# Mixture-of-experts kernel: experts in pairs, full-precision products on column tiles, twelve ring slots

## What is computed

```
h = silu(x @ w_gate) * (x @ w_up)          # x: 80 x 1024, the weights 1024 x 1024, float32
out[rows] += gate * score * (h @ w_down)
```

## Time and profile before

| | |
|---|---|
| median of 3 runs | 2026.26 us (2024.73 to 2031.66) |
| profiled execution | 2036.07 us, span 2034.3 us |
| mean granted clock of TensorE in it | 0.911 of full speed |
| moved by DMA | 519 MB, 255 GB/s over the span |

### The profile page before, as it was taken

The page is one execution under the profiler, slowest core; times in us unless marked ns, Lnnn a source line. Parts: engine busy times, 40 slices in busy tenths (PEclk is TensorE's granted clock), DMA queues, the critical chain, the costliest instruction groups (busy, mean ns, idle before and its releaser), DMA issues.

```text
span 2034.3 us, 24624 instructions
## 1 busy us (share of the span) xinstructions
PE 1811.8 (89%) x8919; PEld 1273.2 (63%) x8919; DVE 1511.7 (74%) x1438; ACT 1144.3 (56%) x1134; POOL 527.7 (26%) x320
## 2 busy tenths in 40 slices
PE   5899789699999999999478799898699999999995
PEld 2788567366666666665257588777466666666663
DVE  2477553599999999998255466635799999999994
ACT  2477621277777777775231235412477777777773
POOL 1223210214343433331210320000123334343332
PEclk8899887699999999999788779796799999999997
DMA  9300726699999999999730510007499999999992
GB/s 387 104 1 1 279 104 234 259 347 379 382 367 380 364 383 368 380 387 345 96 131 1 191 63 2 1 1 303 159 362 374 379 383 368 380 368 383 366 387 61
DMA packets 139901, 519.03 MB, mean 255 GB/s; under 512 B 14943, under 2 KB 15231, under 8 KB 138814
## 3 DMA queue, kind: packets, MB, share of 16 engines
q1 hardware_dynamic: 131248, 488.02, 62.7%
q0 software_dynamic: 7216, 24.79, 6.3%
q10 hardware_dynamic: 1374, 5.37, 0.6%
HBM read 496.90 MB, written 21.24 MB: 255 GB/s over the span
## 4 chain that ended last, share of the span: by engine, by line
PE 65%; DVE 15%; issue 7%; ACT 6%; DMA 4%; SPq 1%; POOL 1%; DVEq 0%; POOLq 0%; ACTq 0%
PE ps L783 25%; PE ps L788 14%; DVE whl L1536 7%; PE ps L739 6%; PE ps L988 4%; ACT whl L1158 3%; PE ps L1035 2%; DMA ring<-in_at_w_qkv 2%; PE ps L1008 2%; PE ps L1024 2%; DMA ring<-in_mod_w 2%; PE ps L719 1%; DVE W L1554 1%; PE ps L892 1%; SPq L353 1%
## 5 line engine op out<-in xcount | busy, mean ns | idle before, releaser
L1536 DVE TENSOR_TENSOR whl<-ring,whl 128x2048 fp32r<-128x2048 f32 x384 | 922.8, 2428 | 84.8 <-ACT whl L1158 81.6
L1158 ACT ACTIVATE whl<-ring 128x2048 fp32r<-128x2048 f32 x384 | 735.8, 1917 | 247.4 <-PE ps L788 247.1
L783 PE MATMUL ps<-whl,xs_hl 128*80 128x512 f32 x2048 | 558.8, 395 | 8.3 <-DVE xs_hl L1560 4.8
L783 PEld LDWEIGHTS ps<-whl,xs_hl 128*80 128x80 f32 x2048 | 299.5, 149 | 168.0 <-issue 7.0
L788 PE MATMUL ps<-whl,xs_hl 128*80 128x512 f32 x1024 | 322.4, 396 | 19.0 <-DVE whl L1536 19.0
L783 PE MATMUL ps<-whl,hs_hl 128*80 128x512 f32 x1024 | 280.8, 396 | 3.4 <-ACT hs_hl L1065 3.4
L788 PEld LDWEIGHTS ps<-whl,xs_hl 128*80 128x80 f32 x1024 | 147.7, 148 | 117.4 <-DVE whl L1536 41.9
L580 POOL TENSOR_TENSOR W<-W 80x1024 f32<-80x1024 f32 x32 | 89.9, 2808 | 495.5 <-ACT W L1196 495.5
L783 PEld LDWEIGHTS ps<-whl,hs_hl 128*80 128x80 f32 x1024 | 153.3, 150 | 89.1 <-ACT hs_hl L1065 3.6
L788 PE MATMUL ps<-whl,hs_hl 128*80 128x512 f32 x512 | 160.8, 396 | 0.0
L574 POOL COPY sg<-g_t 80x1 f32 (+1 forms) x32 | 82.7, 2585 | 189.8 <-DMA x_mid<-W,si 99.1
(11 more groups left out here) (253 smaller groups left out, 2481.9 us busy)
## 6 DMA issues: line engine op xcount, KB each, us to landing
ring<-in_moe_w_gate SPq DMA_DIRECT2D x128, 1024.0 KB, 8.0
ring<-in_moe_w_up SPq DMA_DIRECT2D x128, 1024.0 KB, 7.2
ring<-in_moe_w_down SPq DMA_DIRECT2D x128, 1024.0 KB, 7.2
ring<-in_mod_w SPq DMA_DIRECT2D x48, 1024.0 KB, 9.8
ring<-in_rg_w_in SPq DMA_DIRECT2D x8, 1024.0 KB, 21.9
ring<-in_at_w_qkv SPq DMA_DIRECT2D x8, 768.0 KB, 20.3
x_hat<-r ACTq DMA_DIRECT2D x2, 2560.0 KB, 19.0
ring<-in_rg_w_out SPq DMA_DIRECT2D x4, 1024.0 KB, 9.6
```

Source lines behind the costliest of these rows:

```text
L783: nc.tensor.matmul(ps[0:CE, bank + n, :], xhl[:, part, k, :], w[:, 0, n * 512:(n + 1) * 512], start=(k == 0 and part == 0), stop=False)
L1158: nc.scalar.activation(whl[:, whl_slot(u), 0, :], ring[:, slot, :], ACT.Copy).then_inc(whi_ok, 1)
L1536: v.tensor_tensor(whl[:, whl_slot(u), 1, :], ring[:, n % MSLOTS, :], whl[:, whl_slot(u), 0, :].bitcast(F32), ALU.subtract).then_inc(wlo_ok, 1)
```

## The change

Experts go in pairs (`NP` = 8). The 64 latent rows of two experts stand side by side in PE's 128 weight columns as two tiles of 64, their context rows (16 each) in four tiles of 32, one for each expert and half of the output columns. The products take the ring's weights as they are, in float32; the splits, `whl` and the split rows go, and all 12 slots carry weights. The host orders expert, modulation and output weights so that a slot's row of one partition is 8 KB in one piece. A pair's output is one fused operation on DVE for the latent rows and four for the context rows; POOL scatters in two rounds, one for each expert of a pair, with a wait for the landing after each. The norm weights come as rows of 128 values that POOL expands, the rotary tables and sinks in the partitions' order. The weights for queries, keys and values are loaded into slots 4 to 7 during the last pair and into 0 to 3 after vector 10 of the modulation, which like vector 9 is loaded during the last pair; ACT and DVE split the first four ahead of x, and the product goes in the order 4 to 7, 0 to 3. The core of the diff:

Loads (SP):

```diff
-SLOTS, MSLOTS = 12, 8
-ROUND_RG, ROUND_AT = 1, 5
-MOD_ROUNDS = (0, 2, 3, 4)
+SLOTS = 12
...
+SLOT_LOADS = (("m0", "w_in", "m3", "m6", "moe0", "m10", "qkv", "moe1"),
+              ("m1", "w_in", "m4", "m7", "moe0", "qkv", "moe1"),
+              ("m2", "w_out", "m5", "moe0", "m9", "m8", "w_o", "m11", "moe1"))
+QKV_ORDER = (4, 5, 6, 7, 0, 1, 2, 3)
...
-                def put(slot, w, e, s):
-                    sp.dma_start(pair(slot), w3[w][:, bass.ds(e * KB + 2 * s, 2), :]).then_inc(slot_ready[slot], 16)
...
+                w3 = [w[layer].rearrange("s p n -> p s n") for w in (moe_w_gate, moe_w_up, moe_w_down)]
+                def part(slot, w, e, s):
+                    sp.dma_start(ring[:, slot:slot + 1, :], w3[w][:, bass.ds(e * 4 + s, 1), :]).then_inc(slot_ready[slot], 16)
...
-                def step_loads(e, i, par, more, _):
-                    for n in range(USES):
-                        if not more and not 4 <= n < 8:
-                            continue
-                        m = n if more else n - 4
-                        sp.wait_ge(wlo_ok, e * USES + (ESLOTS * layer + m + 1))
-                        put((4 * par + m) % MSLOTS, (0, 2, 1)[n // 4], e + int(n // 4 != 1), n % 4)
+                    part(slot, int(n >= 16), n % 2, n % 8 // 2)
+                def step_loads(i, par, more, _):
+                    for n in range(0, 24 if more else 8, 2):
+                        what = n // 8 if more else 1
+                        sp.wait_ge(moe_used, i * PAIR_USES + (LAYER_USES * layer + n // 2 + 3))
+                        for a in range(2):
+                            part(n % SLOTS + a, (0, 2, 1)[what], (i + int(what != 1)) * 2 + a, n % 8 // 2)
...
-            sp.wait_ge(x_mid_in, 16)
-            for s in range(KB):
-                load(ROUND_AT, s, ring[:, s, 0:QKV], at_w_qkv[s * P:(s + 1) * P, :])
-            load_mod(8)
+            load_mod(9, moe_used, lambda s: LAYER_USES - 6 + s // 2 + 1)
+            load_mod(10, moe_used, lambda s: LAYER_USES - 4 + s // 2 + 1)
+            def load_qkv(s):
+                sp.dma_start(ring[:, s, 0:QKV], at_w_qkv[s * P:(s + 1) * P, :]).then_inc(slot_ready[s], 16)
+            for s in range(4, KB):
+                sp.wait_ge(moe_used, LAYER_USES - 4 + s // 2 + 1)
+                load_qkv(s)
+            for s in range(4):
+                sp.wait_ge(ring_used, used(10, s))
+                load_qkv(s)
+            load_mod(8, qkv_mm, lambda s: NT)
             sp.wait_ge(qn_ok, NT)
             sp.dma_start(new_k, qn[:, NH * HD:NQK * HD]).then_inc(kv_stored, 16)
             sp.wait_ge(v_ok, NT)
```

Products and turns (PE):

```diff
                 def turn_row(v):
                     pe.wait_ge(mod_row, v + 1)
+                    if v == 8:
+                        pe.wait_ge(ob_ok, 41)
                     if v:
...
+                def product(n0, ready_at, bank, lat, ctx):
+                    for s in range(4):
+                        slots = [(n0 + 2 * s + a) % SLOTS for a in range(2)]
+                        for a in range(2):
+                            pe.wait_ge(slot_ready[slots[a]], ready_at(n0 + 2 * s + a))
+                        for h in range(2):
+                            k = 2 * s + h
                             for n in range(2):
...
+                                cols = slice(h * D + n * 512, h * D + (n + 1) * 512)
+                                for a in range(2):
+                                    nc.tensor.matmul(ps[a * CL:(a + 1) * CL, bank + n, :], lat(a, k), ring[:, slots[a], cols],
+                                                     start=(k == 0), stop=(k == KB - 1))
+                            for q in range(4):
+                                a, n = q // 2, q % 2
+                                mm = nc.tensor.matmul(ps[q * CG:q * CG + CC, bank + 2, :], ctx(a, k),
+                                                      ring[:, slots[a], h * D + n * 512:h * D + (n + 1) * 512],
+                                                      start=(k == 0), stop=(k == KB - 1))
+                        mm.then_inc(moe_used, 1)
+                        yield s
...
+                def x_turn(p, part):
+                    if part == 0:
+                        pe.wait_ge(gathered, p * 32 + 32 * (pb + 1))
+                        for b in range(KB):
+                            mm = nc.tensor.transpose(ps[:, 6 + b // 4, (b % 4) * P:(b % 4 + 1) * P], xg_l[:, b * P:(b + 1) * P], ident[:, :])
+                    elif part == 1:
+                        pe.wait_ge(xt_mul, p * 2 + (2 * pb + 1))
+                        return
+                    else:
+                        w = CG + CC
+                        for b in range(KB):
+                            mm = nc.tensor.transpose(ps[:, 6, b * w:(b + 1) * w], xg_c[0:w, b * P:(b + 1) * P], ident[0:w, 0:w])
                     mm.then_inc(xtr_mm, 1)
...
+                def h_turn(i, part):
+                    pe.wait_ge(h_ok, i * 2 + (2 * pb + part + 1))
+                    if part == 0:
+                        for b in range(KB):
+                            mm = nc.tensor.transpose(ps[:, 6 + b // 4, (b % 4) * P:(b % 4 + 1) * P], hs_l[:, b * P:(b + 1) * P], ident[:, :])
+                    else:
+                        pe.wait_ge(ht_ok, i * 2 + (2 * pb + 1))
+                        for b in range(4):
+                            mm = nc.tensor.transpose(ps[:, 6, b * P:(b + 1) * P], hs_c[:, b * P:(b + 1) * P], ident[:, :])
                     mm.then_inc(htr_mm, 1)
...
+                    for s in down(8 if more else 0, at, y):
+                        if s < 3 and rows_left:
+                            x_turn(i + 2, s)
                     if more:
+                        pe.wait_ge(sil_ok, i * 2 + 2 * (pb + 2))
...
+                x_turn(0, 0)
+                x_turn(0, 1)
+                x_turn(0, 2)
+                pe.wait_ge(ob_ok, 41 * layer + 1)
+                pe.wait_ge(xt_ok, 2 * (pb + 1))
+                for s in gate_up(8, at, 0, 0):
+                    if s < 3:
+                        x_turn(1, s)
+                for _ in gate_up(16, at, 3, 0):
+                    pass
```

Rows, outputs and scatters (DVE, POOL):

```diff
-                v.tensor_copy(g_t[:, :], ps[0:CE, 4, 0:NE]).then_inc(route_ok, 1)
-                v.tensor_copy(idx_t[:, :], ps[0:CE, 4, NE:2 * NE]).then_inc(route_ok, 1)
...
+                found = ps[:, 4, 0:4 * NE].rearrange("p (q e a) -> p q e a", q=4, a=2)
+                v.tensor_copy(to_l[:, :], ps[0:CL, 4, NE:2 * NE]).then_inc(route_ok, 1)
+                v.tensor_copy(to_c[:, :], ps[0:CC, 4, 3 * NE:4 * NE]).then_inc(route_ok, 1)
+                for out, q, half in ((il, 1, CL), (ic, 3, CG), (gl, 0, CL), (gc, 2, CL)):
+                    for a in range(2):
+                        v.tensor_copy(out[a * half:(a + 1) * half, :], found[a * half:(a + 1) * half, q, :, a]).then_inc(route_ok, 1)
...
+                def x_mod(p, buf):
+                    for part, cols, src in ((0, slice(0, 2 * CL), ps[:, 6:8, :].rearrange("p h (m n) -> p (h m) n", m=4)),
+                                            (1, slice(2 * CL, XW), ps[:, 6, 0:KB * (CG + CC)].rearrange("p (k n) -> p k n", k=KB))):
+                        shape = [P, KB, cols.stop - cols.start]
+                        out = xt[:, buf, :, cols]
+                        eng.wait_ge(xtr_mm, p * 2 + (2 * pb + part + 1))
+                        v.tensor_tensor(out, src, mod_scale[:, :, part:part + 1].to_broadcast(shape), ALU.mult).then_inc(xt_mul, 1)
+                        eng.wait_ge(xt_mul, p * 2 + (2 * pb + part + 1))
+                        v.tensor_tensor(out, out, mod_shift[:, :, part:part + 1].to_broadcast(shape), ALU.add).then_inc(xt_ok, 1)
...
+                def output(i, bank, more):
+                    eng.wait_ge(moe_used, i * PAIR_USES + (LAYER_USES * layer + (16 if more else 12)))
+                    eng.wait_ge(sg_ok, i * 4 + 4 * (pb + 1))
+                    v.scalar_tensor_tensor(out=ob_l.rearrange("p (h n) -> p h n", h=2), in0=ps[:, bank:bank + 2, :], scalar=sg_l[:, 0:1],
+                                           in1=gg_l.rearrange("p (h n) -> p h n", h=2), op0=ALU.mult, op1=ALU.mult).then_inc(ob_ok, 1)
+                    for q in range(4):
+                        rows = slice(q * CG, q * CG + CC)
+                        v.scalar_tensor_tensor(out=ob_c[q // 2 * CG:q // 2 * CG + CC, q % 2 * 512:(q % 2 + 1) * 512],
+                                               in0=ps[rows, bank + 2, :], scalar=sg_c[rows, 0:1], in1=gg_c[rows, :],
+                                               op0=ALU.mult, op1=ALU.mult).then_inc(ob_ok, 1)
...
+                def next_rows(p):
+                    if not isinstance(p, int) or p:
+                        pool.wait_ge(gathered, p * 32 + 32 * pb)
+                        pool.wait_ge(xtr_mm, p * 2 + 2 * pb)
+                    nc.gpsimd.tensor_copy(gi_l[:, :], il[:, bass.ds(p, 1)]).then_inc(gi_ok, 1)
```

(97 more changed lines are left out.)

523 lines of the change are left out of this document (199 added, 324 removed).

## The result

The changed kernel takes 2066.26 us (median of four executions, 2059.14 to 2068.19) against 2027.6 us beside it: a ratio of 1.0182, 95% interval 1.0156 to 1.0209, so it is slower by 1.6 to 2.1%. The forecast was 2051 us, slower, range 1942 to 2090. The profiled execution has a span of 2066.4 us, 32.1 more than the one of before. A second series gave 2059.57 us (2057.93 to 2068.36) against 2032.24, a ratio of 1.0145 (1.0125 to 1.0166). Between the medians the change costs 38.7 us in the first series and 27.3 in the second; the forecast had 25.

A forecast was written before the change was run, and what follows sets the result against it. TensorE was taken to bound the kernel, VectorE and DMA close behind. Stages +22, starts +6, between layers -10, tail +9, earlier loads -2 sum to +25 us: 2051 us against the median, range 1942 to 2090.

The forecast's parts named there:

- The step: Expert products on TensorE, per 128 input rows: 2.58 us of passes, 0.20 width changes, 0.09 weight loads; 2.87 us.
- the terms of 0.10 a change and 0.09 for the loads: Expert products: each of two tile-width changes a step costs 0.10 us, uncovered weight loads 0.09 us a step.
- Rival A: Expert products: changing from 64 to 32 columns costs nothing, a step takes 2.58 us; 1955 us in all, chance 0.26.
- B: Expert products: a width change costs 0.10 to 0.12 us including loads, step 2.78 to 2.82; 2015 to 2035 us, chance 0.14.
- C: Expert products: 64-column tiles run one after the other, four more passes a step, +660 us; 2710 us, chance 0.04.
- The stages: Both expert stages: 582 us each against 571 before, +11 a stage, +22 us for both.
- 8 x 72.0, and 6: An expert stage: eight pairs of 72.0 us, plus 6 us nothing covers in the last pair; 582 us.
- POOL's queue and the loads: Expert stages: scatters and gathers take 42 us, covered by 52; weight loads take 62 to 65 us a pair, below 72.
- Rival D: POOL's queue in the expert stages: scatters and gathers need 58 us for 52, 6 a pair; 2145 us, chance 0.04.
- Between the layers: Between the expert stage and query/key/value product: the weight wait goes, x comes next, product starts at 1019.9 for 1030.2; -10 us.
- The starts: Starts of both expert stages: more small copies, a second gather issue, wider multiply and add; about 3 us each, +6.
- the earlier loads: First 12 MiB of modulation weights, before the first routing: 8 KB rows instead of 4 KB load faster; -2 us.

The follow-up runs named there:

- eight passes: Changed kernel with context matmuls given the 64 latent columns as weights, so tile width never changes and a step has eight passes: 2290.9 us, one execution.
- four-step form: Changed kernel with four 128-row steps of latent rows, then four of context rows: 1985.22 us; with TensorE's loop written out too, 1970.74 us.
- eight steps: Changed kernel with all eight 128-row steps of a product's latent rows before its context rows, TensorE's loop written out: 1977.11 us, ratio 0.9749 to the kernel before.

## Why the prediction was right, point by point

- **The step, right.** 2.87 us forecast, 2.85 measured; the tests leave the change of width as the only cause, so the terms of 0.10 a change and 0.09 for the loads hold in their sum (0.29 for 0.27). Which part of 0.135 us is the change itself and which the loads was not separated, so whether each term was right stays open. Rival A's 2.58 and B's 2.78 to 2.82 fall, C falls with eight passes in 3.43 us.
- **The stages, right for the first, short for the second.** 582 us forecast; 579.2, and 590.8. The second has 11.6 us more that no term held: two gaps of 3.9 and 4.2 us at the turn of the loop, and a step at half speed behind each, 5.45 us for 2.85. That makes 13.3, as against 13.9 less with the loop written out; the first stage makes up 1.7 with a step at half speed near its end (3.63 us for 1.94 from 949.16, granted clock 0.54), which the second does not have. The step that failed is "8 x 72.0, and 6", which took the program's own supply for free; the change made TensorE's program longer (75 instruction loads for 41), and no row of before shows such a gap.
- **POOL's queue and the loads, right.** No wait for a gather or the ring in either stage, and 372 GB/s at a share of 0.97. The four-step form later moved 399 at full share, so about 7% was to spare where the forecast had 10. Rival D falls.
- **Between the layers, the sign right and the reason half right.** -10 forecast, -6.2 measured. The step that failed is the first half of "four weight slots come in the last pair and four once vector 10 is done, and the broadcast is short rows, so that wait goes": the early loads win nothing (2060.25 with them late, 2059.57 with them early), and the short rows carry the gain (+15 without them, -18.5 by themselves on the kernel before). I took the broadcast for one of two reasons of the 36.44 us; it was the one that counted. That x comes next and takes 20.3 us from its read to the product was right (1006.89 to 1027.18). The second scatter round was sized at +9 for both ends; here the two rounds end 13.1 us later, since the first one runs beside the early weights (8.77 us for 3.63; with the weights late the two rounds end 6.9 us later), at the tail 9.8.
- **The starts:** +6 forecast for both, +2.5 measured: -1.8 for the first and +4.3 for the second, 3 forecast for each (the terms listed for one add up to 3.4 to 4.4, not 3). In the first the modulation product (L672, from 382.98 us, and L657 behind it) stands between routing and transposes and covers the copies and the gathers: its transposes wait for no gather, those of the second for 8.64 us. The forecast had no such cover.
- **The sum**, 25, fell 7 short of the 32.1 between the two profiled executions: the gaps (+11.6), the stretch between the layers (+3.8) and the terms within 2 (+3.5 in all) against both stages without the gaps (-5.9), the first start (-4.8) and the earlier loads (-1.1). That no more is missing is in part luck: errors of +18.9 and -11.8 offset each other.
- A term that hides in all of these: the stretch of the query/key/value products takes 102.8 us in the first profile and 98.4 in the second of the same kernel, at a granted clock of 0.92 and 0.97. These are 4.4 of the 10.3 us by which the two profiled executions differ.

## What to carry to other kernels

Where tiles of two widths alternate, order the matmuls so that the width changes seldom: the same matmuls gave 2066, 2010 and 1985 us, until a block is so long that slots and copies behind it come late (eight steps, 1977 for 1971). When a transfer ends a chain, look at what runs beside it before moving it: 640 KB of norm weights in small pieces, for 64 KB in rows, cost more than the place of 6 MB of weights. A loop with a long body can wait for its own program at the jump back, and the profile shows that as "issue" and one instruction load.

## What the runs showed of the hardware that was not expected

- The jump back in TensorE's loop cost 3.9 and 4.2 us in the second stage and nothing in the first, for the same body; after each, a step at half the speed (granted clock 0.50).
- The wait for a scatter's landing is 3.6 us on a quiet DMA and 7.6 to 8.8 beside weight loads (between the layers, in the ten profiles with the early weights).
- Two 64-column tiles in full precision share a pass of 0.43 us without a gap, block after block.
